# FFN 1 in the Strassen form of FFN 2, with its modulation sums moved, and the first item of each group split in two parts

## The reference

```python
c_act = silu(c)
mod = (c_act @ w_ada + b_ada).reshape(B, 3, 3, 1024)       # 9 sections of shift, scale, gate
h = modulate(rms_norm(x, g1), mod[:, 0, 0], mod[:, 0, 1])
x = x + 0.5 * mod[:, 0, 2] * ((silu(h @ Wg) * (h @ Wu)) @ w_out)      # FFN 1, 1024 -> 2 x 2816 -> 1024
x = x + mod[:, 1, 2] * mixer(modulate(rms_norm(x, gmix), mod[:, 1, 0], mod[:, 1, 1]))
x = x + 0.5 * mod[:, 2, 2] * swiglu(modulate(rms_norm(x, g2), ...))   # FFN 2, as FFN 1
return rms_norm(x, gfin)
```

## Time and profile before

| what | value |
|---|---|
| three runs | 884.86 us median (884.81 to 887.31) |
| the profiled execution | 886.71 us, of which the span from first to last instruction is 885.0 us |
| TensorE busy | 859.1 us, 97% |
| VectorE, ScalarE, GpSimd busy | 584.4, 332.3 and 36.0 us |
| mean granted clock of TensorE | 0.991 of full speed |
| transfers | 134.46 MB, 152 GB/s on the mean |

### The profile page before, as it was taken

One profiled execution on the slowest core, in us unless ns is written; L12 is line 12 of the kernel. 1 busy time (PEld: TensorE's weight loads), 2 busy tenths in 40 slices (PEclk: granted clock), 3 DMA queues, 4 the chain that ended last, 5 costly groups with the idle time before them and its releaser, 6 DMA issues.

```text
span 885.0 us, 13666 instructions
## 1 busy us (share of the span) xinstructions
PE 859.1 (97%) x5290; PEld 743.5 (84%) x5290; DVE 584.4 (66%) x902; ACT 332.3 (38%) x434; POOL 36.0 (4%) x42
## 2 busy tenths in 40 slices
PE   4999999999999999999999999999999999999996
PEld 3778888888888888897887898899988899999886
DVE  4579777777776756538645469988633588885443
ACT  6232222222223221225424346665521256664323
POOL 0000000000000000000340000000000000100000
PEclk9899999999999999999999999999999999999998
DMA  9977666666656555434533322566343576562322
GB/s 268 289 215 234 191 191 191 192 194 191 194 179 204 160 172 166 146 108 108 142 96 96 94 73 72 139 173 171 85 130 93 118 181 165 148 168 83 99 66 96
DMA packets 219501, 134.46 MB, mean 152 GB/s; under 512 B 5577, under 2 KB 214589, under 8 KB 219453
## 3 DMA queue, kind: packets, MB, share of 16 engines
q1 hardware_dynamic: 216516, 128.52, 50.1%
q0 software_dynamic: 2880, 5.24, 3.7%
q10 hardware_dynamic: 56, 0.01, 0.0%
HBM read 126.41 MB, written 2.10 MB: 145 GB/s over the span
## 4 chain that ended last, share of the span: by engine, by line
PE 90%; DVE 5%; ACT 2%; SPq 1%; DMA 1%; issue 1%; ACTq 0%
PE ps L1569 22%; PE ps L1571 21%; PE ps L1570 21%; PE ps L1948 7%; PE ps L1944 7%; PE ps L1946 7%; PE ps L1826 1%; PE ps L1760 1%; DMA ada_first<-in_w_ada_dram 1%; PE ps L1827 1%; PE ps L1828 1%; DVE h_lo L1021 1%; DVE sw_lo_a L1447 1%; SPq L397 1%; DVE xs L1014 0%
## 5 line engine op out<-in xcount | busy, mean ns | idle before, releaser
L1569 PE MATMUL ps<-h_hi,w_split 128*128 128x512 f32 (+1 forms) x464 | 179.8, 388 | 5.5 <-DVE h_lo L1021 5.3
L1571 PE MATMUL ps<-h_hi,w_split 128*128 128x512 f32 (+1 forms) x464 | 180.0, 388 | 0.0
L1570 PE MATMUL ps<-h_lo,w_split 128*128 128x512 f32 (+1 forms) x464 | 178.9, 386 | 0.0
L968 DVE TENSOR_TENSOR w_split<-w_raw,w_split 128x2048 fp32r<-128x2048 f32 (+1 forms) x45 | 93.3, 2073 | 75.9 <-ACT w_split L610 75.9
L1569 PEld LDWEIGHTS ps<-h_hi,w_split 128*128 128x128 f32 x464 | 87.4, 188 | 26.9 <-issue 4.5
L610 ACT CAST w_split<-w_raw 128x2048 fp32r<-128x2048 f32 (+1 forms) x45 | 77.1, 1714 | 81.8 <-PE ps L1571 72.7
L1570 PEld LDWEIGHTS ps<-h_lo,w_split 128*128 128x128 f32 x464 | 87.6, 189 | 18.4
L1571 PEld LDWEIGHTS ps<-h_hi,w_split 128*128 128x128 f32 x464 | 87.6, 189 | 16.6
L1065 DVE SCALAR_TENSOR_TENSOR ada_acc<-ada_raw,c_act,ada_acc 128x256 f32<-128x256 f32 x196 | 95.1, 485 | 7.0
L1944 PE MATMUL ps<-sums_hi,sw_hi 128*128 128x256 f32 x320 | 89.3, 279 | 0.9 <-DVE sw_lo_a L1447 0.5
L1946 PE MATMUL ps<-sums_lo,sw_hi 128*128 128x256 f32 x320 | 89.6, 280 | 0.0
(11 more groups left out here) (186 smaller groups left out, 1533.2 us busy)
## 6 DMA issues: line engine op xcount, KB each, us to landing
ada_raw<-in_w_ada_dram SPq DMA_DIRECT2D x56, 512.0 KB, 3.6
sw_raw<-in_ffn_w_in_dram SPq DMA_DIRECT2D x100, 256.0 KB, 4.1
w_raw<-in_ffn_w_in_dram SPq DMA_DIRECT2D x47, 512.0 KB, 6.0
ada_first<-in_w_ada_dram SPq DMA_DIRECT2D x16, 512.0 KB, 7.4
w_raw<-in_ffn_w_out_dram SPq DMA_DIRECT2D x16, 384.0 KB, 4.0
w_raw<-in_w_mix_in_dram SPq DMA_DIRECT2D x12, 512.0 KB, 4.3
sw_raw<-in_ffn_w_out_dram SPq DMA_DIRECT2D x16, 384.0 KB, 4.1
w_raw<-in_ffn_w_out_dram SPq DMA_DIRECT2D x16, 320.0 KB, 3.3
```

Of the source, the lines that this page charges most:

```text
L968: nc.vector.tensor_tensor(w_lo[s][:, 0:n], w_raw[s][:, 0:n], w_hi[s][:, 0:n].bitcast(F32), ALU.subtract).then_inc(lo_ready, 1)
L1569: nc.tensor.matmul(dst, w_h, a_h, start=start, stop=False)
L1570: nc.tensor.matmul(dst, w_h, a_l, start=False, stop=False)
L1571: return nc.tensor.matmul(dst, w_l, a_h, start=False, stop=stop)
```

## The change

FFN 1 keeps 8 plain tiles (tiles 0 to 7) and does the other 14 as Strassen tiles, 3 in a first group and 11 in a second, each group followed by 8 down items; it uses the code, the buffers and the semaphores of FFN 2, one set of semaphores for each FFN. `sw_raw` shares memory with `ada_raw` and `w_raw`. The modulation works in 14 units of 512 columns, each in two parts of 4 steps. Parts 0 to 7 stand beside the plain tiles, with two halves of 512 KB in `ada_raw` (two steps each); parts 8 to 19 beside the down items of FFN 1 and 24 to 27 beside those of FFN 2, their data in the free end of `sw_raw` ("hosted", one transfer of 1 MB behind the item's own, with a wait and a semaphore of its own); parts 20 to 23 stand in the mixer. Where a group changes, the first item's first columns are cast and subtracted apart (`cast_down_early`, `cast_up_early`) as soon as TensorE has left those columns. The v weights of the mixer get buffers of their own. Cut to its core:

```diff
+    PLAIN = (8, 2)
+    ADA_PLAIN = {0: (0,), 1: (1, 2), 2: (3,), 4: (4, 5), 5: (6, 7)}
+    HOSTED = ({down_item(0, g, m): 8 + 6 * g + m for g in range(2) for m in range(6)},
+              {down_item(1, 0, m): 24 + m for m in range(4)})
+    def used(part, steps=KD // 2):
+        return part // 2 * LINKS + part % 2 * (KD // 2) + steps
...
@@ SyncE @@
+            def load_ada(part):
+                n = ADA_RAW.index(part)
                 for s in range(2):
+                    if n:
+                        sp.wait_ge(ada_link, used(ADA_RAW[n - 1], (s + 1) * KA // 2))
+                    k0 = part % 2 * KA + s * KA // 2
+                    sp.dma_start(ada_raw[:, s], w_ada_v[:, k0:k0 + KA // 2, ada_cols(part)])\
                       .then_inc(ada_full[s], 16)
...
+            def load_down2(f, g, m):
...
+                sw_free(f, i, False)
...
+                if i in HOSTED[f]:
+                    part = HOSTED[f][i]
+                    k0 = part % 2 * KA
+                    host_free(f, i)
+                    sp.dma_start(host_view(s), w_ada_v[:, k0:k0 + KA, ada_cols(part)]).then_inc(host_full[f][s], 16)
+            for j in range(2, PLAIN[0]):
+                load_pair(ffn1_w_in, j, j % 2, UP1 + j)
+                for part in {2: (0,), 3: (1, 2), 4: (3,), 5: (4,), 6: (5, 6), 7: (7,)}.get(j, ()):
+                    load_ada(part)
+            sp.wait_ge(ada_link, used(7))
+            for n in range(N0[0]):
+                load_up(0, n)
+            for m in range(KD):
+                load_down2(0, 0, m)
+            for n in range(N0[0], NS[0]):
+                load_up(0, n)
...
@@ ScalarE @@
+            def cast_down_early(f, g):
+                i = down_item(f, g, 0)
+                act.wait_ge(sw_used[f], pieces(f, i) - 2)
+                act.wait_ge(sw_full[f][i % 2], landed(f, i))
+                nc.scalar.copy(down_hi(0)[:, 0:EARLY_K * P], sw_raw[:, i % 2, 0:EARLY_K * P]).then_inc(early_hi[f], 1)
...
+            for j in range(PLAIN[0]):
+                plain_silu(0, j)
+                if j == 0:
+                    split_hi_part(2, 0)
+                    split_hi_part(2, 1)
+                elif j + 2 < PLAIN[0]:
+                    split_hi(j + 2)
+                if j == 2:
+                    plain_hi(0, j)
+                if j in (2, 3):
+                    for r in (2 * j - 4, 2 * j - 3):
+                        hsum_split(0, r)
+                if j != 2:
+                    plain_hi(0, j)
+                if j == PLAIN[0] - 2:
+                    for c in range(3):
+                        cast_up(0, 0, c)
...
@@ VectorE @@
+            def ada_steps(part, raw_of, full_of):
+                u, k0 = part // 2, part % 2 * KA
+                acc, turned = work[:, 3, :], work[:, 4, :]
+                for q in range(KA):
+                    k = k0 + q
+                    if u or k:
                         dve.wait_ge(ada_link, u * LINKS + k)
+                    full, count = full_of(q)
+                    dve.wait_ge(full, count)
                     if k == 0:
+                        ins = nc.vector.tensor_scalar(acc, raw_of(q), c_act[:, 0:1], None, ALU.mult)
                     else:
+                        ins = nc.vector.scalar_tensor_tensor(acc, raw_of(q), c_act[:, k:k + 1], acc, ALU.mult,
+                                                             ALU.add)
                     ins.then_inc(ada_link, 1)
+                if part % 2:
...
+            for j in range(PLAIN[0]):
+                plain_product(0, j)
+                if j == 0:
+                    for part in range(2):
+                        split_lo_part(2, part)
+                elif j + 2 < PLAIN[0]:
+                    split_lo(j + 2)
+                if j == 3:
+                    hsum_2(0)
+                    hsum_4(0)
+                    hsum_rest(0, 2)
+                    hsum_rest(0, 3)
+                plain_lo(0, j)
+                for part in ADA_PLAIN.get(j, ()):
+                    ada_own(part)
+                if j == 2:
+                    shift_difference(0)
+                    hsum_1(0)
+                    hsum_3(0)
+                    hsum_rest(0, 0)
+                    hsum_rest(0, 1)
+                elif j == PLAIN[0] - 2:
+                    add_blocks(0, 0)
+                    rest_up(0, 0, 0)
+                    rest_up(0, 0, 1)
+                elif j == PLAIN[0] - 1:
+                    rest_up(0, 0, 2)
+            up_group(0, 0)
...
@@ TensorE @@
+            def down2(f, g, m, between=None):
+                if m:
+                    pe.wait_ge(sw_lo_ready[f], pieces(f, down_item(f, g, m)) + 1)
+                else:
+                    pe.wait_ge(early_lo[f], 3 if g else 1)
...
+                for k in range(GF):
+                    if m == 0:
+                        b_tile(f, g, k)
+                        if k == EARLY_K:
+                            pe.wait_ge(sw_lo_ready[f], pieces(f, down_item(f, g, 0)) + 1)
...
+            for j in range(3, PLAIN[0]):
+                pe.wait_ge(prod_ready, j - 1)
+                pair(j % 2, UP1 + j, (2 * (j % 2), 2 * (j % 2) + 1), h_hi, h_lo)
+            for n in range(N0[0]):
+                strassen(0, n)
+            sum_units(0)
+            for m in range(KD):
+                down2(0, 0, m)
+            for n in range(N0[0], NS[0]):
+                strassen(0, n)
```

More of the change, by code:

```diff
@@ L761, in _ @@
+            first_group(0)
+            for n in range(N0[0], NS[0]):
+                up_slot(0, n)
+            for m in range(KD - 1):
+                cast_down(0, 1, m + 1)
+                if m == 0:
+                    product_hi(0, NS[0] - 1)
+                    nc.scalar.activation(dummy, ones[:, 0:1], ACT.Sqrt)
+                square(m, 0)
+            split_hi(MIXIN)
+            act.wait_ge(sq_added, KD)
             square_half(KD - 1, 0, 1, 0)
@@ L1537, in _ @@
-            for n in range(N0):
-                up_slot(n)
+            split_lo_part(UP2 + 1, 0)
+            hsum_1(1)
+            split_lo_part(UP2 + 1, 1)
+            add_blocks(1, 0)
+            plain_product(1, 0)
+            hsum_rest(1, 0)
+            rest_up(1, 0, 0)
+            hsum_3(1)
+            hsum_2(1)
+            rest_up(1, 0, 1)
+            hsum_rest(1, 2)
+            hsum_rest(1, 1)
+            hsum_4(1)
+            rest_up(1, 0, 2)
+            plain_lo(1, 0)
+            hsum_rest(1, 3)
@@ new lines, in down2_half @@
+            def down2_half(m, half, between=None):
+                cols = HALVES[half]
+                hi, lo = (v.rearrange("p (k n) -> p k n", n=P) for v in (down_hi(m), down_lo(m)))
+                for k in range(GF):
+                    if between:
+                        between(k)
+                    ins = product(ps[:, LAST_BANK[half], cols], hi[:, k, :], lo[:, k, :], b_hi[:, k, cols],
+                                  b_lo[:, k, cols], k == 0, k == GF - 1)
+                ins.then_inc(last_done, 1)
@@ new lines, in _ @@
+            pe.wait_ge(prod_ready, 1)
+            plain(0, 2)
+            for j in range(3, PLAIN[0]):
[4 more added lines that the diff above has]
+            sum_units(0)
+            for m in range(KD):
+                down2(0, 0, m)
+            for n in range(N0[0], NS[0]):
+                strassen(0, n)
+            for m in range(KD - 1):
+                if m == KD - 2:
+                    sum_units(1)
+                down2(0, 1, m)
@@ L2028, in transposes @@
+            for n in range(N0[1], NS[1]):
+                strassen(1, n)
             def transposes(k):
```

1427 lines of the change are left out of this document (664 added, 763 removed).

## The result

The changed kernel takes **901.81 us** (median of 4 runs, 900.6 to 902.2) against 884.84 us (884.42 to 887.31): a ratio of 1.0184, 95% interval 1.0163 to 1.0205. It is 17.0 us slower; 4.7 were forecast and the range ended at 896. The profiled execution has a span of 900.5 us against 885.0, 15.5 more; the other 1.5 us are that the profiled execution of before stood 1.85 us above its median and this one 0.4. Later runs of the kernel before have medians of 886.6 us, so the 15.5 us between the spans are likely the better size of the loss.

The account below looks back on a forecast made before the run. TensorE, busy 97% of the span, was taken as the bound. 19.7 (chain) + 2.0 (clock) + 0.3 (shifts) - 17.3 (tiles and waits) = +4.7 us, median 889.6 us; range 879 to 896, likeliest case 886 to 893.

Parts of the forecast that it names:

- Fourteen tiles: FFN 1: fourteen tiles go from 10.98 us plain to 9.89 us Strassen, saving 15.3 us.
- FFN 2's waits: FFN 2's group changes: three TensorE waits, with slower first matmuls after two of them, go away, saving 2.0 us.
- nothing charged at FFN 1's group changes: FFN 1's new group changes: the same early casts guard them, so no cost was added.
- The chain: Plain tiles: weights and modulation parts wait on each other; TensorE loses 0.6, 2.8, 8.0 and 8.3 us, 19.7 in sum.
- The clock: Behind the second 8 us idle stretch: a low clock for up to 7 us costs 0 to 3.5 us, 2.0 taken.
- After the first the loss is hidden: Behind the first 8 us idle stretch: low clock costs nothing, since VectorE and transfers set the next start.
- It is covered: FFN 1's down items: VectorE's work, at most 7.3 us an item, fits beside TensorE's 7.5 us, so no cost.
- the mixer's entry: Before the mixer: the v weights' subtraction ahead of the last update costs 0 to 1 us; 0.3 taken with small shifts.
- Parts 20 to 23 fall into the mixer's waits: Mixer: modulation parts 20 to 23 run in waits already there, at no charge.
- what lies beside other work: Down items, mixer and mixer's entry: added work is covered or falls into waits; 0.3 us charged in all.
- The third rival: FFN 1's groups: late transfers and FFN 2's hosted parts add some 6 us, 895.6 us; chance 0.13 for 893 to 900.
- The two rivals with a faster kernel: Plain tiles wait less: 882.2 us, chance 0.17 for 878 to 887; waits not there at all: 867.9 us, chance 0.10.

Follow-up runs that it names:

- e8_noearly: The kernel of e5_all with the early parts undone, so each group's first item is cast and subtracted whole in both FFNs: 887.83 us.
- e2_ring: The changed kernel with a second buffer for the odd modulation parts 1, 3, 5 and 7; first Strassen transfers wait for part 6, not 7: 885.38 us.
- e5_all: The changed kernel with weights ahead of modulation parts on SyncE, a second modulation buffer, earlier mixer transfers, and ScalarE's second split of sums behind tile 5's cast: 880.92 us.
- e12_plain: The changed kernel with only the three plain-stage edits (order of the weights, second modulation buffer, ScalarE's order), nothing behind it touched: 882.23 us.
- e6_vload: The kernel of e5_all with the mixer's first weights (2 MB) sent behind down items 6 and 7 instead of between items 4 and 5: 876.45 us.
- e7_best: The kernel of e6_vload with part 7 hosted at down item 6, part 6 in own memory, first Strassen sums behind part 6, mixer's first weights split earlier: 873.63 us.
- e11_down: The changed kernel, plain stage untouched, with only later edits: mixer's first weights sent later and split earlier, its other transfers sent earlier: 898.24 us.
- e4_mixer: The changed kernel with the mixer's third and fourth weight blocks no longer waiting for the split of the first two: 900.19 us.

## Why the prediction was wrong

The direction and the main mechanism were right. The size was not: +4.7 us forecast, +15.5 measured between the spans. By its own steps:

- *Fourteen tiles, 15.3 us.* Right. The eleven tiles of the second group ran from 240.74 to 348.50 us, 9.80 us each, 1.0 us better in sum than 9.89.
- *FFN 2's waits, 2.0 us; nothing charged at FFN 1's group changes.* Right: FFN 2 takes 2.2 us less (342.6 to 340.4), and e8_noearly shows the six waits that the early parts keep away.
- *The chain, 19.7 us.* The mechanism was right, and e2_ring, e5_all and e12_plain show it: with the chain cut, the first stage is 16 to 21 us shorter. The size came out at 23.7: the first Strassen tile started at 146.38 where 56.77 + 6 x 10.98 = 122.65 was possible. The waits were 1.62, 2.59, 7.89 and 6.72 us against 0.6, 2.8, 8.0 and 8.3, 18.8 in sum; the other 4.9 us are tiles that took longer at a lower clock (tile 7 2.8, tiles 5 and 6 1.6), which the chain hides: followed back from 146 us to tile 2, the chain of work that ended last holds no step of TensorE. The first Strassen tile started 3.3 us later than forecast. The chain was on time until 105.6; it lost 1.4 us at the second half of part 5, 0.4 at tile 7's pair and 1.5 at part 7, as a half of `ada_raw` landed in 4.8 us in the median here (3.6 taken) and a transfer of a pair in 6.9. The other 0.7 us are that tile 2 started earlier.
- *The clock, 2.0 us.* The step held and its size was near. "After the first the loss is hidden" is right: tile 7 lost 2.8 us and delayed nothing. Behind the start of Strassen the clock was 0.72 over 9.62 us, which is 5.4 us at 0.50 and costs 2.7. The row behind the bound of 7 us was read too short: it is the middle of a longer low stretch of the kernel before (0.62 from 19.40 to 22.00 us, 0.50 to 29.00, 0.79 to 32.00). What the sum had at nothing is the second piece of the first Strassen tile, 1.48 us at 153.33, where ScalarE's cast had to wait for GpSimd's adding transfer (148.40) with the `ev` copy behind it. The first three Strassen tiles took 34.1 us instead of 29.7, 4.4 more: +2.4 us.
- *"It is covered" (the down product) and the mixer's entry, 0.3 us.* Wrong: 67.25 + 60.24 us against 124.55 before, 2.9 us. Of these 1.85 are 2 MB of mixer weights ahead of an item's weights on SyncE's queue (e6_vload), which I had not walked past this stage, and 0.88 stand at the mixer's entry. I had put the latter down to the split ahead of the last update; with the split moved ahead, e7_best and e11_down still wait 0.75 and 0.72, so the cause of most of it stays open. A candidate that no run isolates: the 7.3 us of VectorE an item left out its two waits for ScalarE (0.70 and 0.57 us), and in the second group of the changed kernel an item took it 7.02 and, with the transpose, 8.73 us (from 386.63 to 393.65 and to 402.38), 15.75 for two where TensorE takes 15.1. +2.6 us.
- *"Parts 20 to 23 fall into the mixer's waits", 0.* Wrong, the largest step that I had at nothing: part 20 and the weights in front of it brought the spatial weights 1.87 us later than TensorE wanted them. The mixer lost 3.7 us in the profiled execution, and e4_mixer gives all of it back; 1.1 to 1.9 us are the order, the rest is the cold clock behind the wait, which this execution had and five others did not.
- *Start.* Tile 2 started 0.7 us earlier than in the earlier trace rows, which is the execution, not the change.

Together: 4.7 + 4.0 + 2.4 + 2.6 + 3.7 - 1.0 - 0.2 - 0.7 = 15.5 us. The step that failed is the part "what lies beside other work": I costed it by VectorE's work and the rate of transfers, and its two losses, 6.3 us more than I had charged, sit in the order of one queue (1.85 us and the mixer's 3.7, with the clock behind its wait) but for the 0.88 us at the mixer's entry. The chain, 4.0 us too small, and the start of Strassen with its clock, 2.4, are mis-sized terms. The third rival, FFN 1's groups lose as well, had the right sign for the wrong reason.

The two rivals with a faster kernel were not idle ones. The change is worth what it takes away once the queues are in order: e7_best is 1.4%, about 13 us, below the kernel before, of 17.3 us that the steps add up to.
